# Two-layer decoder trunk: norm sums on VectorE with one ones-product, finer weight waits, and a last norm by token

## The reference

```python
def layer_norm(x, g, b, eps=1e-5):
    mu = jnp.mean(xf, -1, keepdims=True)
    var = jnp.mean(jnp.square(xf - mu), -1, keepdims=True)
    return (xf - mu) * lax.rsqrt(var + eps) * g + b

xp = layer_norm(ALPHA * xp + yp, ln_g[layer, 0], ln_b[layer, 0])
xp = layer_norm(ALPHA * xp + swiglu(xp, w_ffn_gate[layer], w_ffn_up[layer], w_ffn_down[layer]),
                ln_g[layer, 1], ln_b[layer, 1])
```

## Time and profile before

| | |
|---|---|
| median of 3 runs | 3721.32 us (3720.71 to 3721.37) |
| profiled execution | 3722.03 us, with a span of 3720.2 us |
| TensorE busy | 3443.2 us, 93% of the span |
| VectorE, ScalarE, GpSimd busy | 1238.5, 708.6, 1015.7 us |
| mean granted TensorE clock | 0.939 of full speed |

### The profile page before, as it was taken

One profiled execution on the slowest core, in us unless ns is written; L12 is line 12 of the kernel. 1 busy time (PEld: TensorE's weight loads), 2 busy tenths in 40 slices (PEclk: granted clock), 3 DMA queues, 4 the chain that ended last, 5 costly groups with the idle time before them and its releaser, 6 DMA issues. The chain is left out here.

```text
span 3720.2 us, 55802 instructions
## 1 busy us (share of the span) xinstructions
PE 3443.2 (93%) x22142; PEld 3136.8 (84%) x22142; DVE 1238.5 (33%) x2450; ACT 708.6 (19%) x1426; POOL 1015.7 (27%) x546
## 2 busy tenths in 40 slices
PE   8998778998989769999999999998879999999997
PEld 7997556676766559999999998997659999999996
DVE  6713545555555432200004215113652300003123
ACT  1101333433434321200001102101230200001002
POOL 3542111101112024222223342321335122233231
PEclk9999889998999869999999999998769999999999
DMA  3112332323233570111111112110122011111111
GB/s 128 50 45 56 105 108 80 94 75 88 77 84 84 147 254 24 35 45 45 46 52 43 47 45 74 47 49 24 52 71 78 25 53 48 45 45 43 47 47 46
DMA packets 327225, 246.83 MB, mean 66 GB/s; under 512 B 28336, under 2 KB 321977, under 8 KB 325356
## 3 DMA queue, kind: packets, MB, share of 16 engines
...
...
## 5 line engine op out<-in xcount | busy, mean ns | idle before, releaser
L556 PE MATMUL ps<-X_rounded,c_w_hi 128*128 128x344 f32 x2712 | 872.7, 322 | 10.2 <-issue 7.2
L558 PE MATMUL ps<-X_rounded,c_w_rounded 128*128 128x344 f32 x2712 | 869.5, 321 | 0.0
L557 PE MATMUL ps<-c_xla,c_w_hi 128*128 128x344 f32 x2112 | 675.5, 320 | 0.0
L556 PEld LDWEIGHTS ps<-X_rounded,c_w_hi 128*128 128x128 f32 x2712 | 510.7, 188 | 12.3 <-issue 7.7
L502 POOL CAST c_w_hi<-c_w 128x2048 fp32r<-128x2048 f32 (+2 forms) x101 | 156.5, 1550 | 1322.8 <-DMA c_w<-in_w_ffn_up 763.4
L558 PEld LDWEIGHTS ps<-X_rounded,c_w_rounded 128*128 128x128 f32 x2712 | 510.2, 188 | 0.0
L557 PEld LDWEIGHTS ps<-c_xla,c_w_hi 128*128 128x128 f32 x2112 | 399.0, 189 | 0.4
L504 POOL TENSOR_TENSOR c_w_rounded<-c_w,c_w_hi 128x2048 fp32r<-128x2048 f32 (+2 forms) x101 | 378.9, 3751 | 8.1
L556 PE MATMUL ps<-c_f_hi,c_w_hi 128*128 128x344 f32 x1056 | 343.6, 325 | 13.1 <-DVE c_f_lo L931 13.1
L558 PE MATMUL ps<-c_f_hi,c_w_rounded 128*128 128x344 f32 x1056 | 341.2, 323 | 0.0
L557 PE MATMUL ps<-c_f_lo,c_w_hi 128*128 128x344 f32 x1056 | 339.6, 322 | 0.0
...
## 6 DMA issues: line engine op xcount, KB each, us to landing
...
```

What stands on the lines that cost most here:

```text
L556: pe.matmul(dst, whi, xhi, start=first, stop=False)
L557: pe.matmul(dst, whi, xlo, start=False, stop=False)
L558: return pe.matmul(dst, wlo, xhi, start=False, stop=last)
```

## The change

1. **Means.** VectorE gets `total(nm, c, m, ...)`, two additions of 344 columns for each column block that add feature tiles 6 and 7 onto `sums`; `mean` is one ones-product instead of three. This holds for three norms: both `na`, and `nb` of layer 0.
2. **Variances.** VectorE gets `fold(nm, c)`, one `tensor_reduce` over the eight feature blocks of the squares (read with the block index innermost); `variance` is then one ones-product instead of eight. It is used for all three blocks of both `na`, and for block 0 of `nb` in layer 0. Blocks 1 and 2 of that `nb` keep the eight products.
3. **First products by block.** Each of the eight `low` instructions raises `low_ready`, and the first chunk on a fresh column block waits for them one by one (`fresh`). `seq_up` now goes (0,0), (1,0), (0,1), (1,1), (0,2), (1,2). `mean` and `variance` are put inside chunks. In `na`, `scale` and `low` of block 2 move behind the first two `hide` on VectorE, and ScalarE does two Silu before the third inverse root, with its table loaded again.
4. **Weights.** Gate and up weights of a unit are fetched with a wait each (on `gated` and on `upped`) and split by two pairs of POOL instructions of 1,024 columns each; the first of their products waits for its own half.
5. **Last norm.** In layer 1 the raw residual is transposed token tile by token tile (`turn`), eight products with one column of `ones_d` give the mean of each token (`row_mean`), ScalarE squares and sums a token's row in one pass, and VectorE does the rest by rows (`centre_row`, `shape`, `settle`) with gain and bias spread over all partitions; four stage buffers in place of two. Five of the nine tiles are turned before the last down chunk.

```diff
-    seq_up = [(0, 0), (1, 0), (0, 1), (0, 2), (1, 1), (1, 2)]
+    seq_up = [(m, c) for c in range(NB) for m in range(2)]
...
             def fetch_up(n):
-                if n >= 2:
-                    sp.wait_ge(upped, {2: 4, 3: 6}.get(n, 3 * (n - 1)))
                 for part, (_, src) in enumerate(up_src(n)):
+                    if n >= 2:
+                        sp.wait_ge(upped if part else gated, {2: 5, 3: 6}.get(n, 3 * (n - 1)))
                     b = 16 * (n % 2) + KD * part
-                    sp.dma_start(raw[:, b:b + KD, :], src).then_inc(w_in_u[n % 2], 16)
+                    sp.dma_start(raw[:, b:b + KD, :], src).then_inc(w_in_u[n % 2][part], 16)
...
-                b = slice(16 * (n % 2), 16 * (n % 2) + 16)
-                split(w_in_u[n % 2], 32 * (n // 2 + 1), w_split_u, n, hi[:, b], raw[:, b], lo[:, b])
+                for part in range(2):
+                    b = slice(16 * (n % 2) + KD * part, 16 * (n % 2) + KD * part + KD)
+                    split(w_in_u[n % 2][part], 16 * (n // 2 + 1), w_split_u, 2 * n + part, hi[:, b], raw[:, b], lo[:, b])
...
+            def mean(nm, c):
+                sums = sums_a if nm is na else sums_b
+                pe.wait_ge(nm.totalled, 2 * c + 2)
                 if c:
                     pe.wait_ge(nm.centred, c)
-                pe.matmul(r.ps[:, 6, 0:CW], r.ones_d[:], sums[:, c, :], start=True, stop=False)
-                pe.matmul(r.ps[:, 6, 0:CW], r.ones_d[:], r.X[:, 6, cols(c)], start=False, stop=False)
-                pe.matmul(r.ps[:, 6, 0:CW], r.ones_d[:], r.X[:, 7, cols(c)], start=False,
-                          stop=True).then_inc(nm.mean_ready, 1)
+                pe.matmul(r.ps[:, 6, 0:CW], r.ones_d[:], sums[:, c, :], start=True, stop=True).then_inc(nm.mean_ready, 1)
 
             def variance(nm, c):
-                pe.wait_ge(nm.squared, c + 1)
                 if c:
                     pe.wait_ge(nm.logged, c)
+                if nm is na or c == 0:
+                    sums = sums_a if nm is na else sums_b
+                    pe.wait_ge(nm.folded, c + 1)
+                    pe.matmul(r.ps[:, 7, 0:CW], r.ones_d[:], sums[:, c, :], start=True, stop=True).then_inc(nm.var_ready, 1)
+                    return
...
-            out(6, 1)
-            mean(na, 0, evicted_o, 20)
+            out(6, 1, range(4))
+            mean(na, 0)
+            out(6, 1, range(4, KD))
             out(7, 1)
-            out(6, 2)
+            out(6, 2, range(5))
             variance(na, 0)
-            mean(na, 1, evicted_o, 22)
+            out(6, 2, range(5, KD))
+            mean(na, 1)
             out(7, 2)
...
+            def up(m, slot, c, bank, part, fresh=False):
                 for k in range(KD):
+                    if fresh:
+                        pe.wait_ge(na.low_ready, KD * c + k + 1)
...
             for s, (m, c) in enumerate(seq_up):
-                pe.wait_ge(na.low_ready, c + 1)
                 if s < 3:
                     pe.wait_ge(evicted_o, (21, 23, 24)[s])
                 else:
                     pe.wait_ge(hidden, s - 2)
+                if s < 2:
+                    pe.wait_ge(w_split_u, 4 * m + 2)
+                up(m, m, c, s % 3 * 2, 0, m == 0)
                 if s == 1:
-                    pe.wait_ge(w_split_u, 4)
-                up(m, m, c, s % 3 * 2, 0)
+                    variance(na, 1)
+                if s < 2:
+                    pe.wait_ge(w_split_u, 4 * m + 4)
+                up(m, m, c, s % 3 * 2, 1)
                 if s == 0:
-                    mean(na, 2, evicted_o, 24)
-                    variance(na, 1)
-                if s == 1:
+                    mean(na, 2)
+                if s == 2:
                     variance(na, 2)
...
+            def turn(n):
+                rows = tiles[n][1]
+                pe.wait_ge(evicted_d, (44, 44, 46, 46, 46, 48, 48, 48, 48)[n])
+                if n in user:
+                    pe.wait_ge(row_shaped, user[n] + 1)
+                for k in range(KD):
+                    mm = pe.transpose(r.ps[0:rows, tile_bank[n] + k // 4, k % 4 * P:(k % 4 + 1) * P],
+                                      r.X[:, k, n * P:n * P + rows], r.ident[:])
+                mm.then_inc(turned, 1)
+                if n:
+                    pe.wait_ge(row_centred, n)
+                for k in range(KD):
+                    mm = pe.matmul(r.ps[0:rows, 0, n:n + 1], r.X[:, k, n * P:n * P + rows], r.ones_d[:, 0:1],
+                                   start=(k == 0), stop=(k == KD - 1))
+                mm.then_inc(row_mean, 1)
...
+                down_chunk(14, 1, range(4))
+                mean(nb, 0)
+                down_chunk(14, 1, range(4, KH))
+                down_chunk(15, 1)
+                variance(nb, 0)
+                down_chunk(14, 2, range(4))
+                mean(nb, 1)
+                down_chunk(14, 2, range(4, KH))
+                down_chunk(15, 2)
+                variance(nb, 1)
+                mean(nb, 2)
+            else:
+                down_chunk(14, 1)
+                turn(0)
+                down_chunk(15, 1)
+                turn(1)
+                down_chunk(14, 2, range(4))
+                turn(2)
+                down_chunk(14, 2, range(4, KH))
+                turn(3)
+                turn(4)
+                down_chunk(15, 2)
+                for n in range(5, 9):
+                    turn(n)
...
+            act.preload_act_table_set("natural_log_exp_and_others")
+            square(na, 0)
+            inverse_root(na, 0)
+            finish(na, 0)
+            square(na, 1)
+            inverse_root(na, 1)
+            square(na, 2)
+            finish(na, 1)
+            for s in range(2):
+                light(s, s % 3 * 2)
+            act.preload_act_table_set("natural_log_exp_and_others")
+            inverse_root(na, 2)
+            finish(na, 2)
+            for s in range(2, 6):
...
+                for n, (_, rows) in enumerate(tiles):
+                    got = r.ps[0:rows, tile_bank[n]:tile_bank[n] + 2, :].rearrange("p b n -> p (b n)")
+                    act.wait_ge(turned, n + 1)
+                    act.wait_ge(row_centred, n + 1)
+                    act.activation(junk[0:rows, :], got, ACT.Square, bias=row_stat[0:rows, n, 0:1],
+                                   accum_out=row_stat[0:rows, n, 1:2]).then_inc(row_squared, 1)
+                    act.wait_ge(row_squared, n + 1)
+                    act.activation(row_stat[0:rows, n, 2:3], row_stat[0:rows, n, 1:2], ACT.Ln, bias=r.bias[0:rows, 0:1],
+                                   scale=1 / D).then_inc(row_logged, 1)
+                    act.wait_ge(row_logged, n + 1)
+                    act.activation(row_stat[0:rows, n, 2:3], row_stat[0:rows, n, 2:3], ACT.Exp,
+                                   scale=-0.5).then_inc(row_rstd, 1)
...
+            def total(nm, c, m, evicted, need, n):
+                sums, summed = (sums_a, summed_a) if nm is na else (sums_b, summed_b)
+                v.wait_ge(evicted, need)
+                if m == 6:
+                    v.wait_ge(summed, 13 + c)
+                else:
+                    v.wait_ge(nm.totalled, n)
+                v.tensor_tensor(sums[:, c, :], sums[:, c, :], r.X[:, m, cols(c)], ALU.add).then_inc(nm.totalled, 1)
+
+            def fold(nm, c):
+                sums = sums_a if nm is na else sums_b
+                v.wait_ge(nm.squared, c + 1)
+                v.tensor_reduce(sums[:, c, :], nm.rows[:, :, cols(c)].rearrange("p k n -> p n k"), AX.X,
+                                ALU.add).then_inc(nm.folded, 1)
...
+                def shape(n):
+                    rows = tiles[n][1]
+                    got = r.ps[0:rows, tile_bank[n]:tile_bank[n] + 2, :].rearrange("p b n -> p (b n)")
+                    v.wait_ge(row_squared, n + 1)
+                    if n == 0:
+                        v.wait_ge(rows_in, 32)
+                    if n >= 4:
+                        v.wait_ge(stored[n % 4], 16 * (n // 4))
+                    v.scalar_tensor_tensor(out=stage[0:rows, n % 4, :], in0=got, scalar=row_stat[0:rows, n, 0:1],
+                                           in1=g_row[0:rows, :], op0=ALU.add, op1=ALU.mult).then_inc(row_shaped, 1)
+
+                def settle(n):
+                    rows = tiles[n][1]
+                    v.wait_ge(row_rstd, n + 1)
+                    v.wait_ge(row_shaped, n + 1)
+                    v.scalar_tensor_tensor(out=stage[0:rows, n % 4, :], in0=stage[0:rows, n % 4, :],
+                                           scalar=row_stat[0:rows, n, 2:3], in1=b_row[0:rows, :], op0=ALU.mult,
+                                           op1=ALU.add).then_inc(row_settled, 1)
```

266 lines of the change are left out of this document (130 added, 136 removed).

## The result

The changed kernel takes 3680.67 us (median of 4 runs, 3678.41 to 3690.19), the kernel before beside it 3721.02 (4 runs): a ratio of 0.9909, 95% interval 0.9887 to 0.993. That is 40 us less, where 53 were forecast. The profiled execution has a span of 3676.6 us against 3720.2.

What follows compares the result with a forecast made beforehand. TensorE's list of work was taken to bound the chain phases. Terms of 14.5 + 13.5 - 3.4 + 10.2 + 20 - 1.5 = 53.3 us off 3722.0, with the median 0.7 lower, gave 3668 us, range 3654 to 3691.

Steps and rivals of the forecast that it cites:

- TensorE's list: Chain phases: TensorE's work sets the time; a mean loses 1.16 us per block, a variance 4.05, each `na` 15.6.
- new waits: First norm of layer 0: TensorE waits 2.9 us before variance 0, 1.1 before block 0, 2.9 before block 1.
- two signs: Wrong if: fold of 4 us or more; matmuls 0.295 us apart in chunk (15,2) and turns of 5 us.
- I take 3.0, the row of the same size: VectorE's fold of 2,752 columns was put at 3.0 us, like the centring; 4.2 us as bound from above.
- rival 1: The fold is slow because of its 4,128-byte step: far end 6.0 us per fold, 21 us in all, 3689; chance 0.15.
- the tail: Last norm, tile turns around the last down chunks: end at 3699 to 3700, 20 us less, 1.5 taken off for clock.
- Hidden with 3 us to spare: Unit 2's gate half, asked for three chunks (11.4 us) ahead, arrives in time; without this cover up to 3 us a layer.
- The clock: Behind the four new waits of 2.9 us, half a clock loss each, 0.85 us, 3.4 us in all.
- Rival 2: The clock falls to half in the tail, one-column products leaving the array idle: 8 to 13 us, 3678; chance 0.2.
- Rival 4: Slower, by one fold long enough: the 53 us are gone at 12 us per fold; chance 0.02.
- rival 5: No change to be told, by folds of 11 us each; chance 0.02.
- Rival 3: The new waits hold no clock loss and the tail keeps its clock: 5 us better, 3663; chance 0.2.

Runs made afterwards that it cites:

- experiment 1: The changed kernel with twelve more reductions behind the last `settle`, inner steps from 4 to 4,128 bytes; single run 3734.14 us; 3.00 us at 4 bytes, 5.02 from 16 on.
- experiment 5: The changed kernel unedited, run again on another chip: 3682.16 us beside 3711.74 for the kernel before, ratio 0.9924.
- Experiment 2: The changed kernel with the fold as three additions of adjacent columns in place of one reduction: 3664.01 us beside 3711.98 for the kernel before, ratio 0.9869.
- experiment 7: The changed kernel with the first products of a column block waiting for all eight low halves: 3696.51 us, ratio 0.9964 to the kernel before.
- experiment 8: The changed kernel with gate and up weights of a unit fetched behind one wait and split as one: 3697.18 us, ratio 0.9959 to the kernel before.
- experiment 12: The changed kernel with 30 unused products filling TensorE's wait for the first fold of each first norm: 3682.94 us, ratio 0.992 to the kernel before.
- Experiment 6: The changed kernel with a tile's row means in the last norm as one product over added-up sums: 3669.08 us, ratio 0.9887 to the kernel before.

## Why the prediction came out as it did

The mechanism was right in its parts: TensorE's list shrank, and new waits of the named kinds came where they were put. One term was mis-sized, and two signs that the prediction itself gave for being wrong came up: a fold of over 4 us and a turn of 5 us.

**The fold was mis-sized, and this was the only large error.** "I take 3.0, the row of the same size" is the step that failed. It measured 5.33, above the 4.2 I had as its upper bound and short of rival 1's 6.0; experiment 1 gives the reason, rival 1's, a step of 4,128 bytes, though any step from 16 bytes on would do. The row that I leaned on for the bound (L2736, 14 ns more for 32 columns) pointed the right way, with 0.44 ns per column of surcharge; experiment 1 has 0.73 ((5.02-3.00)/2,752). Rival 1 had the right mechanism at chance 0.15. By its exchange rate, 6 us for each us of fold, 2.33 us more cost 14.0 us. In the traces the three norms with folds fell short of the forecast by 15.9 us (18.9 for 34.8), so the rate was near.

That 53.3 less 14.0 is 39.3 and the medians moved by 40.3 is in part luck. In the two traces the 43.6 us are made of the 53.3, less 15.9 in those norms and 0.8 in the tail, plus 3.8 at the two starts of the down projection and 3.2 in unchanged code. The forecast had neither of the last two; and on the chip of experiment 5 the gain was 30 us.

Experiment 2 takes the 2.3 us off and gives back 0.40 to 0.55% of the time against the changed kernel on two other chips, 15 to 20 us, against the 14 worked out. The intervals are some 0.3% wide to either side. In the traces the two first norms are 7.4 and 4.1 us shorter.

**TensorE's list** shrank: one product of two records per mean and variance. PE's busy time fell by 47.0 us (3443.2 to 3396.2), of which the forecast had counted 38.7 in the three norms and left the last norm to its own sum.

**The new waits** came where they were put. Before variance 0 it was 5.0 us for 2.9, longer by the fold. Before block 1 it was 2.7 in layer 0 and 1.2 in layer 1 for 2.9, before block 0 0.3 and 1.2 for 1.1. Not forecast were those at variance 1 (2.1) and 2 (1.0), and 2.5 in the second norm, where a fold of 3.0 would have ended with the chunk beside it. **First products per block** were right and large: experiment 7 shows 14 us for them.

**Weights.** "Hidden with 3 us to spare" held (the gate half of unit 2 was split by 1524.9 in layer 0, and TensorE came to it near 1529), and the thin cover was real: experiment 8 takes the separate fetch away and the wait comes.

**The clock.** I took 0.85 us for each of four waits, 1.7 in each first norm. It fell in both layers behind the 5.0 us wait, and by experiment 12 this one fall cost 1.8 us in each; experiment 2 has 3.3 us for two falls in one norm. So the price of a norm was about right, for a wait that was longer. Against that, the down projection's start gained 2.3 and 1.5 us that no term had: before, the windows from 2005 to 2015 us had a granted clock of 0.88 and 0.50; after, the same work at 1995 to 2005 had 0.69 and 0.97, though TensorE waited about as long for the low halves of f (6.5 us before, 6.3 after; in layer 1 even 6.6 and 7.9). That is seen in the traces; no experiment isolates it.

**The tail** came out nearly as summed, 17.7 for 18.5. From the add of chunk (14,1) to the end of the last add 29.4 us pass, 29.5 in the sum, and 22.3 from there to the end, where the sum had some 19 and 1.5 for the clock. Rival 2 holds in a small part: turn 7 lost 2.4 us, turn 6 0.4, and chunk (15,2) nothing. Experiment 6 shows what the forecast passed over: eight one-column products were 1.6 of a turn's 2.6 us, the dearest item of TensorE's list there.

**Small slips.** Two sums are a tenth off: 7.5 + 2.3 + 0.5 is 10.3, and 17 matmuls at 0.295 in place of 0.158 us lose 2.3 us. Nothing rests on it.

**Rival 4** fell, and so did **rival 5**. **Rival 3** had the clock kept in both places; it dropped in both.
